# Held-back gate tiles and a stepwise retention projection between the small S5 output products, and a different activation table at the norms

## What is computed

```python
h = rms_norm(x, norm1_g)
q, k, v, g_ret, u, g_s5 = jnp.split(h @ w_in, SPLITS, axis=-1)
...
o = (inner + cross).reshape(B, L, H, DV)          # 8 heads of 128
mu = jnp.mean(o, axis=-1, keepdims=True)
var = jnp.mean(jnp.square(o - mu), axis=-1, keepdims=True)
ret = ((o - mu) * lax.rsqrt(var + EPS)) * gn_g * jax.nn.silu(g_ret)
...
y = jax.nn.gelu(y)                                # y: the S5 output, 512 x 1024
y = y * jax.nn.sigmoid(y @ glu_w + glu_b)
x = x + jnp.concatenate([ret, y * jax.nn.silu(g_s5)], axis=-1) @ w_out
```

## Time and profile before

| | us |
|---|---|
| median of three runs | 1992.2 |
| the profiled execution | 1996.91 |
| its span in the profile | 1995.1 |
| TensorE matmuls busy | 1895.3 (95%) |
| TensorE weight loads busy (beside the matmuls) | 1537.1 (77%) |
| VectorE busy | 1072.9 (54%) |
| ScalarE busy | 775.2 (39%) |
| GpSimd busy | 487.0 (24%) |

### The profile page before, as it was taken

One profiled execution on the slowest core, in us unless ns is written; L12 is line 12 of the kernel. 1 busy time (PEld: TensorE's weight loads), 2 busy tenths in 40 slices (PEclk: granted clock), 3 DMA queues, 4 the chain that ended last, 5 costly groups with the idle time before them and its releaser, 6 DMA issues.

```text
span 1995.1 us, 23150 instructions
## 1 busy us (share of the span) xinstructions
PE 1895.3 (95%) x8986; PEld 1537.1 (77%) x8986; DVE 1072.9 (54%) x1097; ACT 775.2 (39%) x814; POOL 487.0 (24%) x636
## 2 busy tenths in 40 slices
PE   4899999989998999998999999989999999999998
PEld 3788887867885778776888888777988767887867
DVE  6455555468887986446233343567533527446542
ACT  3222222245666855236334332553233423133342
POOL 0411110033999370020000000300107991100100
PEclk8999999999998999998999999999999996699999
DMA  8465555522243224322323233535814321352411
GB/s 302 137 195 173 185 169 157 155 93 85 84 126 127 74 95 148 126 85 64 105 91 98 85 108 87 146 116 192 169 54 156 96 68 46 101 173 90 152 43 43
DMA packets 202773, 239.43 MB, mean 120 GB/s; under 512 B 5611, under 2 KB 184587, under 8 KB 201547
## 3 DMA queue, kind: packets, MB, share of 16 engines
q1 hardware_dynamic: 185643, 171.27, 26.9%
q0 software_dynamic: 13888, 54.57, 9.3%
q10 hardware_dynamic: 3168, 12.58, 1.7%
HBM read 221.10 MB, written 17.30 MB: 119 GB/s over the span
## 4 chain that ended last, share of the span: by engine, by line
PE 70%; POOL 9%; DVE 7%; ACT 6%; issue 5%; DMA 1%; SPq 1%; DVEq 0%; POOLq 0%; ACTq 0%
PE ps L2025 22%; PE ps L2214 16%; PE ps L2091 9%; POOL conv_out L481 8%; PE ps L2055 4%; ACT w_hi L603 3%; PE ps L2352 2%; PE ps L2393 2%; PE ps L2530 2%; DVE w_lo L1163 2%; DVE ada_acc L1263 2%; PE ps L2443 1%; PE ps L2431 1%; PE ps L2402 1%; DMA w_raw<-in_ffn_w_gate 1%
## 5 line engine op out<-in xcount | busy, mean ns | idle before, releaser
L1163 DVE TENSOR_TENSOR w_lo<-w_raw,w_hi 128x2048 fp32r<-128x2048 f32 x158 | 369.7, 2340 | 577.2 <-ACT w_hi L603 574.9
L603 ACT ACTIVATE w_hi<-w_raw 128x2048 fp32r<-128x2048 f32 x156 | 298.4, 1913 | 684.3 <-PE ps L2214 235.5
L2025 PE MATMUL ps<-u_hi,w_hi 128*128 128x512 f32 x704 | 279.8, 397 | 5.1 <-DVE w_lo L1163 5.0
L2025 PE MATMUL ps<-u_lo,w_hi 128*128 128x512 f32 x704 | 276.2, 392 | 0.0
L2025 PE MATMUL ps<-u_hi,w_lo 128*128 128x512 f32 x704 | 276.0, 392 | 0.0
L2214 PE MATMUL ps<-u_hi,w_hi 128*128 128x512 f32 x656 | 256.9, 392 | 5.0 <-DVE w_lo L1163 5.0
L2214 PE MATMUL ps<-u_lo,w_hi 128*128 128x512 f32 x656 | 255.8, 390 | 0.0
L2214 PE MATMUL ps<-u_hi,w_lo 128*128 128x512 f32 x656 | 255.8, 390 | 0.0
L481 POOL TENSOR_TENSOR conv_out<-conv_out,conv_tap 128x512 f32<-128x512 f32 x120 | 195.4, 1628 | 92.9 <-ACT conv_tap L745 75.9
L2025 PEld LDWEIGHTS ps<-u_hi,w_hi 128*128 128x128 f32 x704 | 133.7, 190 | 37.1 <-issue 7.5
L2025 PEld LDWEIGHTS ps<-u_lo,w_hi 128*128 128x128 f32 x704 | 133.7, 190 | 28.6 <-issue 1.0
(11 more groups left out here) (498 smaller groups left out, 3198.4 us busy)
## 6 DMA issues: line engine op xcount, KB each, us to landing
w_raw<-in_w_in SPq DMA_DIRECT2D x44, 1024.0 KB, 5.1
ada_raw<-in_ada_w POOLq DMA_DIRECT2D x56, 512.0 KB, 5.1
w_raw<-in_ffn_w_gate SPq DMA_DIRECT2D x22, 1024.0 KB, 5.3
w_raw<-in_ffn_w_up SPq DMA_DIRECT2D x22, 1024.0 KB, 5.3
w_raw<-in_ffn_w_down SPq DMA_DIRECT2D x32, 704.0 KB, 4.5
ada_first<-in_ada_w SPq DMA_DIRECT2D x8, 1024.0 KB, 14.3
w_raw<-in_w_out SPq DMA_DIRECT2D x8, 1024.0 KB, 5.1
w_raw<-in_rnn_w_proj SPq DMA_DIRECT2D x4, 1024.0 KB, 5.2
```

The source lines that it names most:

```text
L603: A(WHI[:, slot], WRAW[:, slot], ACT.Copy).then_inc(s["w_hi"], 1)
L1163: V.tensor_tensor(WLO[:, slot], WRAW[:, slot], WHI[:, slot].bitcast(F32), ALU.subtract).then_inc(s["w_lo"], 1)
L2025: ins = M(PS[:, 2 * j + t, 0:n], w[:, j, at_:at_ + P], a[:, k, 0:n], start=(k == 0 and q == 0), stop=(k == KT - 1 and q == 2))
```

## The change

The 24-matmul gate tiles are cut into parts of some steps of k (`gate_part`). Heads 1 to 7 get half a tile each instead of a whole one; the rest (half of tile 5, tiles 6 and 7) is run one step at a time, three wide matmuls, behind every second group of `toeplitz` and `states` products. `ret_part` does the same with `wout_r`: its first chunk goes between the products of `states(2)` and `toeplitz(3)`, half of its second between those of `states(3)`. The S5 products start with `toeplitz(0)`, `states(0)`, `toeplitz(1)`, and y's batches use PSUM banks 4 to 7 alone. ScalarE and VectorE get a new order to match. Apart from this, three of the four early dummies at the norms ask for Ln in place of Exp.

```diff
-        Y_BANK = (0, 4, 6, 4)
+        Y_BANK = (4, 6, 4, 6)
...
-                A(EPSC[:, 4 + c:5 + c], EPSC[:, 1:2], ACT.Exp)
+                A(EPSC[:, 4 + c:5 + c], EPSC[:, 1:2], ACT.Ln)
...
-            A(EPSC[:, 5:6], EPSC[:, 1:2], ACT.Exp)
+            A(EPSC[:, 5:6], EPSC[:, 1:2], ACT.Ln)
...
-            A(EPSC[:, 6:7], EPSC[:, 1:2], ACT.Exp)
+            A(EPSC[:, 6:7], EPSC[:, 1:2], ACT.Ln)
...
             ca_batch(0)
+            ca_batch(1)
             dve.wait_ge(s["rroot"], 1)
             V.reciprocal(RSTDH[:], RSTDH[:]).then_inc(s["rn"], 1)
-            ca_batch(1)
             finish(0)
             finish(1)
-            ca_batch(2)
+            lo_step("gret", 1, 2, 0)
             finish(2)
             finish(3)
+            ca_batch(2)
+            for h in range(4):
+                ret_lo(h)
+            for h in (4, 6):
+                finish(h)
+                finish(h + 1)
+                ret_lo(h)
+                ret_lo(h + 1)
+            lo_step("gret", 1, 2, 1)
             ca_batch(3)
-            for h in range(4, HEADS):
-                finish(h)
...
-            gate_tile(0)
+            gate_part(0, 0, KT)
             scores(0)
-            gate_tile(1)
+            gate_part(1, 0, KT)
...
             for h in range(1, HEADS):
+                gate_part(2 + (h - 1) // 2, (4, 0)[h % 2], (8, 4)[h % 2])
                 if h + 1 < HEADS:
-                    gate_tile(h + 1)
                     scores(h + 1)
                 head_output(h)
                 variance(h - 1)
...
-                if b == 3:
-                    pe.wait_ge(s["y_gelu"], 2)
+                if b >= 2:
+                    pe.wait_ge(s["y_gelu"], b - 1)
...
+            def ret_part(j, k):
+
+                if k == 0:
+                    pe.wait_ge(s["w_lo"], CB["wout_r"] + j + 1)
+                    pe.wait_ge(free[0], UB["wout_r"])
+                    pe.wait_ge(free[1], UB["wout_r"])
+                pe.wait_ge(s["rl"], HEADS if j else k + 1)
+                for t in range(2):
+                    for q, (w, a) in enumerate(((WHI, UH), (WHI, UL), (WLO, UH))):
+                        at_ = 256 * k + P * t
+                        ins = M(PS[:, 2 * j + t], w[:, j, at_:at_ + P], a[:, k],
+                                start=(k == 0 and q == 0), stop=(k == KT - 1 and q == 2))
+                if k == KT - 1:
+                    ins.then_inc(s["mm"], 1)
...
-            toeplitz(0)
+            toeplitz(0, lambda k: gate_part(5, 4 + k, 5 + k))
             variance(HEADS - 1)
-            toeplitz(1)
-            states(0)
+            states(0, lambda k: gate_part(6, k, k + 1))
+            toeplitz(1, lambda k: gate_part(6, 4 + k, 5 + k))
             spread(0)
             spread(1)
-            pe.wait_ge(s["o_ready"], HEADS)
-            toeplitz(2)
-            states(1)
+            states(1, lambda k: gate_part(7, k, k + 1))
             spread(2)
             spread(3)
-            states(2)
+            pe.wait_ge(s["o_ready"], HEADS)
+            toeplitz(2, lambda k: gate_part(7, 4 + k, 5 + k))
             spread(4)
             spread(5)
-            toeplitz(3)
-            states(3)
+            states(2, lambda k: ret_part(0, k))
             spread(6)
             spread(7)
-            pe.wait_ge(s["y_gelu"], 1)
-            gemm("wout_r", 2, UH, UL, ready=lambda k: (s["rl"], k + 1))
+            toeplitz(3, lambda k: ret_part(0, 4 + k))
+            states(3, lambda k: ret_part(1, k))
+            for k in range(4, KT):
+                ret_part(1, k)
+            gemm_chunk("wout_r", 1, 0, UH, UL)
+            gemm_chunk("wout_r", 1, 1, UH, UL)
```

More of the change, by code:

```diff
@@ L1013, in _, with gate_silu, head @@
             decay_load(1)
-            for h in range(HEADS):
-                act.wait_ge(*((s["mm"], CB["gret"] + h // 2 + 1) if h % 2 else (s["gate_mm"], h // 2 + 1)))
-                A(SGR[h][:], PS[:, h % 2], ACT.Silu).then_inc(free[h % 2], 1)
-                if h % 2:
-                    hi_step("gret", h // 4, 2, h // 2 % 2)
+            def gate_silu(f):
+                act.wait_ge(*((s["mm"], CB["gret"] + f // 2 + 1) if f % 2 else (s["gate_mm"], f // 2 + 1)))
+                A(SGR[f][:], PS[:, f % 2], ACT.Silu).then_inc(free[f % 2], 1)
+            def head(h):
                 act.wait_ge(s["pv_mm"], h + 1)
@@ L1026, in _ @@
                 A(RSQ[:], PS[:, PV_BANK[h % 2]], ACT.Square).then_inc(s["rsq"], 1)
+            gate_silu(0)
+            gate_silu(1)
+            hi_step("gret", 0, 2, 0)
+            head(0)
+            head(1)
+            gate_silu(2)
+            head(2)
+            head(3)
+            gate_silu(3)
+            hi_step("gret", 0, 2, 1)
+            head(4)
+            head(5)
+            gate_silu(4)
+            head(6)
+            head(7)
+            gate_silu(5)
             toeplitz(1)
@@ L1039, in y_evac @@
                   ACT.Gelu_apprx_tanh).then_inc(s["y_gelu"], 1)
+            y_evac(0)
+            hi_step("gret", 1, 2, 0)
+            gate_silu(6)
             toeplitz(2)
-            y_evac(0)
-            ret_hi(0)
-            ret_hi(1)
+            y_evac(1)
+            gate_silu(7)
+            for h in range(4):
+                ret_hi(h)
             toeplitz(3)
-            y_evac(1)
-            ret_hi(2)
-            ret_hi(3)
-            y_evac(2)
+            hi_step("gret", 1, 2, 1)
             ret_hi(4)
             ret_hi(5)
-            y_evac(3)
+            y_evac(2)
             ret_hi(6)
             ret_hi(7)
+            hi_step("wout_r", 0, 2, 0)
+            y_evac(3)
             def glu_hi(first, last):
@@ L1851, in _ @@
             decayed(0)
-            for h in range(HEADS):
-                if h % 2:
-                    lo_step("gret", h // 4, 2, h // 2 % 2)
-                if h + 1 < HEADS:
-                    decayed(h + 1)
+            decayed(1)
+            lo_step("gret", 0, 2, 0)
+            for h in range(2, 6):
+                decayed(h)
+            lo_step("gret", 0, 2, 1)
+            decayed(6)
+            decayed(7)
             dve.wait_ge(s["pv_mm"], HEADS)
@@ L2383, in scores, with gate_part @@
                 ins.then_inc(s["sc_mm"], 1)
-            def gate_tile(f):
+            def gate_part(f, first, last):
                 n, j, t = f // 2, f // 2 % 2, f % 2
-                pe.wait_ge(s["w_lo"], CB["gret"] + n + 1)
-                pe.wait_ge(free[t if f >= 2 else 0], UB["gret"] + f // 2)
-                q = 0
-                for k in range(KT):
-                    for w, a in ((WHI, UH), (WHI, UL), (WLO, UH)):
+                if first == 0:
+                    pe.wait_ge(s["w_lo"], CB["gret"] + n + 1)
+                    pe.wait_ge(free[t if f >= 2 else 0], UB["gret"] + f // 2)
+                for k in range(first, last):
+                    for q, (w, a) in enumerate(((WHI, UH), (WHI, UL), (WLO, UH))):
                         at_ = 256 * k + P * t
-                        ins = M(PS[:, t], w[:, j, at_:at_ + P], a[:, k], start=(q == 0), stop=(q == 3 * KT - 1))
-                        q += 1
-                ins.then_inc(s["mm"] if t else s["gate_mm"], 1)
+                        ins = M(PS[:, t], w[:, j, at_:at_ + P], a[:, k], start=(k == 0 and q == 0), stop=(k == KT - 1 and q == 2))
+                if last == KT:
+                    ins.then_inc(s["mm"] if t else s["gate_mm"], 1)
             def head_output(h):
@@ L2432, in toeplitz, with states @@
                                 start=(r == 0), stop=False, skip_group_check=True)
-                ins.then_inc(s["mb_used"], 1)
-            def states(b):
+                    if r == 7:
+                        ins.then_inc(s["mb_used"], 1)
+                    if r % 2:
+                        dense(r // 2)
+            def states(b, dense):
                 if b == 0:
@@ L2445, in states @@
                                     skip_group_check=True)
-                ins.then_inc(s["y_mm"], 1)
+                    if r == 7:
+                        ins.then_inc(s["y_mm"], 1)
+                    if r % 2:
+                        dense(r // 2)
+            def ret_part(j, k):
[5 more added lines that the diff above has]
+                for t in range(2):
+                    for q, (w, a) in enumerate(((WHI, UH), (WHI, UL), (WLO, UH))):
+                        at_ = 256 * k + P * t
[3 more added lines that the diff above has]
+                    ins.then_inc(s["mm"], 1)
             def spread(h):
```

9 lines of the change are left out of this document (4 added, 5 removed).

## The result

The changed kernel took 2003.35 us (median of 11 runs, 1999.31 to 2023.36), the kernel before 1990.84 us (11 runs, 1983.94 to 1996.63). Ratio 1.0087, 95% interval 1.0068 to 1.0106: **slower by 0.9%**, outside the range that was given. The granted clock, averaged over a whole run, has a median of 0.964 in these runs of the change; in the 48 runs of before that stand beside e1 to e4 and e9 to e11 it is 0.964 too. One minus the clock, times the span, is the time lost to the half clock: 72 us in either kernel. The profiled execution of the change took 2003.3 us, its span is 2001.3.

A forecast was written before the change was run, and what follows sets the result against it. TensorE was taken as the bound, at half clock in one stretch. GLU gain 9.0 plus norms 0.6 made 9.6: profiled run 1996.9 to 1987.3, or 1982.6 against the median 1992.2; range 1976 to 1998.

The forecast's parts named there:

- The likeliest case: The forecast proper, chance 0.58: full clock where wide matmuls stand between small products; 9.6 us faster, own range 1977 to 1988.
- the clock holds through the mixed stretch: TensorE's granted clock stays 1.00 from 1642 to about 1705, one window at 0.8 allowed; chance 0.58.
- 4.3 us of loss: Taken off the gain for half clock behind TensorE waits: 1.7 at fourth coefficients, 1.7 in GLU, half of one more.
- The heads: Retention heads, all windows at clock 1.00; seven half gate tiles there start the first toeplitz 13.4 earlier, at 1642.1.
- the gain of 9.0: Gain at the start of the GLU, 13.3, after 4.3 taken off for half clock behind waits.
- Rival A: Clock falls at a pair of spreads, first near 1664, slowing wide matmuls too: 1997, 5 slower; chance 0.30.
- The clock pays for them: Before the last states product, 28.6 us of added wide work is paid by full clock: 1716.4 against 1719.5.
- the gain of 13.3: GLU gemm starts near 1755.8 to 1756.1 instead of 1769.4, before taking off half clock behind waits.
- The other waits: TensorE waits 3.4 for the fourth coefficients, some 4 for the x reload plus addition, 5 to 8 at the first GLU matmul.
- the trip of y: GpSimd stores y and loads it back, ScalarE casts: 31.3 us from the x reload, setting the GLU start.
- Rival B: Clock holds, but the y trip or a late coefficient eats the gain: 1988; GLU over 40 us behind last states; chance 0.12.
- The norms: Early dummy asks for Ln, so the load ahead of root goes in all four norms: 0.6 us, bounds 0 and 1.

The follow-up runs named there:

- e1: The changed kernel with the spreads' two operands grown from 8 rows to 128: median 1991.24 us, ratio to before 1.0003.
- e4: The changed kernel with wide matmuls in one block behind each toeplitz and states instead of dealt out between groups: 1982.70 us, ratio to before 0.9962.
- e9: The changed kernel with wide work in blocks, fourth coefficients earlier, y stored in four batches, spreads at 8 rows: 1973.02 us, ratio to before 0.9900.
- e11: The kernel before with spreads of 32 rows, 24 of them zero, instead of 8: 1989.30 us, ratio to before 0.9995.
- e2: The kernel before with only the three early norm dummies asking for Ln in place of Exp: 1993.47 us, ratio to before 1.0013.

## Why the prediction was wrong

**The likeliest case.** The step that failed is "the clock holds through the mixed stretch", which I gave 0.58 because the retention heads, with small products in them, were at 1.00. The clock fell at 1663.6 and stayed down for 41.0 us, and 58.0 us in all were at half clock where I had taken off 4.3 us of loss, 8.6 at half clock. The heads were the wrong likeness. In the heads of before half of the time went to whole gate tiles; behind 1638 the wide matmuls came by threes between groups of 64 rows and 64 columns, and then 1.9 us of 8 rows. e1 (rows) and e4 (blocks) show that it took both differences: with one of them mended, 58.0 us at half clock become 20.6 or 23.8, and the median clock of all runs goes from 0.964 to 0.971 or 0.970.

**The profile that the gain was counted from.** The sum took the profiled run of before down by 9.6, to 1987.3, and then took the same 9.6 off the median. e1, where the long stretch is gone, has 1987.08 in its profiled run, almost that figure, and yet a median of 1991.24, no better than before. The profiled run of before had 64.8 us at half clock in the very stretch that was to be mended, e2 and e11 have 51.2 in the same order: 13.6 less, which is 6.8 us of time. Most of the gain of 9.0 was an excess of that one run, which the median doesn't have. That 1987.3 and 1987.08 agree is luck in part, since the profiled run of e1 is the second fastest of its 12.

**Rival A happened, nearly step for step.** First pair at 1659.7 and fall at 1663.6 (said: about 1664), `states(1)` with its gate half 12.4 (12.8), pair 3.8 (3.8), `toeplitz(2)` 12.3 (13.0), last y product 1734 (1736), GLU at 1774.8 (1775.4). The stretch began 4 us earlier than I had it (1638.1, not 1642.1), so by distance A was some 3 us too short. Its end figure, 1997, is still 6 under the median. The traces differ by 6.2 us of span, as A had it, but two accidents of the profiled runs hide in that: the profiled run of before stood 6 us above the median of its 11 runs, and the changed kernel's run was ahead by 4 us at norm 3 already (`root` at 1280.2, before at 1284.2), from short half-clock stretches that it didn't have (in the window 1275 to 1285 the clock is 0.83 before and 1.00 after). By the distance, 136.6 stands against 127.3 of the profile of before and against 121.1 in e2: 9 to 16 us.

**"The clock pays for them."** This sentence carried the gain of 13.3, and the clock paid nothing: 0.964 in the median on both sides. In e1, where it pays, the last y product stands 80.2 us behind the first `toeplitz` product; I had 74.3 (1642.1 to 1716.4). Of the 5.9 between, 1.0 had come up by the start of `states(3)` (67.3 us, I had 66.3) and 4.9 came within it (12.9 for 8.0), since its first 10 us ran at half clock behind the wait for the fourth coefficients. For the stretches behind waits I took 4.3 us in all; in e1 they were 20.6 us long, so 10.3 lost. A change between kinds of product is 0.3 in `states` and nothing in `toeplitz`, where I had 0.1 in each: 14.1 us for one of both, I had 13.6. My sum from 1642.1 to the third coefficients is also 1 us too long as added up (its terms give 1682.9, not 1683.9), and they are then 0.8 late, not in time; e1 waits 1.21 there. The other waits were right: 3.74, 3.82 and 3.90 in e1 where I had 3.4, some 4 and 5 to 8. So was the trip of y, 32.2 us from reload to cast in the change against 31.3.

**Rival B**, the clock held and the waits eat it, is close to what e1 shows: 1991 where B had 1988, and the GLU 40.0 us behind the last `states` products, B's sign being more than 40.

**What was right.** The heads: `toeplitz(0)` starts 13.4 earlier, once the 4 us of lead are taken off (1655.5 - 1638.1 = 17.4). `states` at full clock, bounded between 3.4 and 6.9 and taken as 3.6, takes 3.7. The recurrence is in time. The projection of 43 us is 192 wide matmuls of `wout_r`, four chunks of 48, not the two that the section on the kernel before names. The norms: the loads ahead of `root` gone as told, and nothing to measure.

**The Trainium skill's rule** (TensorE: Matmul & The Clock Gate, Part 1: The HAM clock gate), that the clock follows how busy the engine was, agrees with the idle windows (1720, 1740 and 1770 above, at 0.83, 0.83 and 0.66). It does not tell e1 from the change, which are both busy 10.00 of 10 us between 1660 and 1680, at 1.00 and at 0.68 and 0.50.
